# Two MoE stages at batch 1: raw-stream routers, split gather and sums, and the second expert pair's first 4 MB in the dense ring

## The reference, cut to what matters

```python
hn = rms_norm(h, norm_ffn[i])
h = h + hier_moe(hn, ...)
# hier_moe: group router top-1 of 4, expert router top-2 of the 8 in that group
p_group = softmax(xf @ wr_g + br_g);  pg, gi = top_k(p_group, 1)
e_logits = (xf @ wr_e + br_e).reshape(T, 4, 8)
e_in = e_logits of group gi;  pv, pi = top_k(softmax(e_in), 2)
gates = pg * pv / sum(pv)
# every chosen expert e, on its tokens x:  y = (silu(a) * b) @ w_down[e],  a, b = split(x @ w_gu[e])
# out[token] = sum over its two experts of gate * y
```

## Time and profile before

| | |
|---|---|
| median of 3 runs | 2223.04 us (2218.72 to 2226.03) |
| the profiled execution | 2214.99 us |
| its span, first to last instruction | 2213.1 us |
| first MoE stage, from the first `project` to the sums' end | 951.19 to 1434.74 us |
| second MoE stage, the same | 1712.05 to about 2193.8 us |
| PE, share of the span | 94% |
| granted TensorE clock, mean | 0.982 of 2.4 GHz |

### The profile page before, as it was taken

How to read it: one execution, slowest core, us unless ns; L and a number is a source line. 1 busy time by engine, 2 the same in 40 slices (tenths; PEclk the granted TensorE clock), 3 DMA queues, 4 the chain that set the end, 5 groups by cost and what they waited for, 6 DMA issues and landing times.

```text
span 2213.1 us, 38037 instructions
## 1 busy us (share of the span) xinstructions
PE 2089.7 (94%) x15784; PEld 1525.4 (69%) x15785; DVE 892.3 (40%) x1468; ACT 669.1 (30%) x958; POOL 79.6 (4%) x118
## 2 busy tenths in 40 slices
PE   7997899998999998989999999999998999999998
PEld 5876899988999897844454444588987444444444
DVE  5866678745643544521111111165275111111112
ACT  3434464253652466311111111144342011111111
POOL 0100111101000200000000000000000000000000
PEclk9998999999999999999999999999999999999999
DMA  9731389803655251779999999535631899999993
GB/s 361 262 129 48 139 306 333 317 31 115 228 176 187 77 191 41 288 287 421 422 422 422 422 422 422 226 115 190 247 148 77 356 419 422 422 422 422 422 422 126
DMA packets 108084, 603.26 MB, mean 273 GB/s; under 512 B 10062, under 2 KB 10500, under 8 KB 58836
## 3 DMA queue, kind: packets, MB, share of 16 engines
q1 hardware_dynamic: 95872, 559.39, 63.9%
q0 software_dynamic: 11840, 42.34, 5.3%
q10 hardware_dynamic: 276, 0.13, 0.0%
HBM read 600.73 MB, written 1.05 MB: 272 GB/s over the span
## 4 chain that ended last, share of the span: by engine, by line
PE 88%; DVE 4%; ACT 4%; issue 2%; DMA 2%; SPq 0%; DVEq 0%; ACTq 0%
PE bank L939 20%; PE bank L951 10%; PE bank L551 10%; PE bank L552 10%; PE bank L553 10%; PE bank L923 6%; PE bank L970 5%; PE bank L581 4%; DMA dense_w<-in_w_in 1%; PE bank L561 1%; PE bank L562 1%; PE bank L560 1%; PE bank L594 1%; PE bank L631 1%; DVE work L1514 1%
## 5 line engine op out<-in xcount | busy, mean ns | idle before, releaser
L939 PE MATMUL bank<-expert_w,work 128*32 128x512 f32 (+1 forms) x4032 | 447.7, 594 | 24.0 <-issue 21.5
L939 PEld LDWEIGHTS bank<-expert_w,work 128*32 128x32 f32 (+1 forms) x4032 | 156.1, 110 | 314.2 <-issue 314.2
L434 DVE TENSOR_TENSOR w_low<-dense_w,w_high 128x2048 fp32r<-128x2048 f32 x112 | 256.1, 2290 | 221.5 <-ACT w_high L427 220.8
L427 ACT ACTIVATE w_high<-dense_w 128x2048 fp32r<-128x2048 f32 x120 | 228.6, 1911 | 312.1 <-DMA dense_w<-in_mlp_w 195.1
L951 PE MATMUL bank<-expert_w,work 128*32 128x512 f32 (+1 forms) x2016 | 226.4, 594 | 0.0
L2075 DVE TENSOR_TENSOR work<-work,bank 128x512 f32<-128x512 f32 x32 | 22.0, 688 | 400.3 <-ACT work L1404 400.3
L951 PEld LDWEIGHTS bank<-expert_w,work 128*32 128x32 f32 (+1 forms) x2016 | 63.5, 110 | 144.5 <-issue 144.5
L923 PEld LDWEIGHTS bank<-work 128*128 128x128 f32 x1088 | 133.1, 199 | 33.9 <-issue 33.8
L551 PE MATMUL bank<-u_pairs_mlp,w_high 128*128 128x256 f32 x512 | 145.2, 284 | 6.0 <-ACT u_pairs_mlp L1140 6.0
L923 PE MATMUL bank<-work 128*128 128x128 f32 x1088 | 139.2, 287 | 6.9 <-issue 6.9
L551 PE MATMUL bank<-hidden_pairs,w_high 128*128 128x256 f32 x512 | 144.9, 283 | 0.0
(11 more groups left out here) (379 smaller groups left out, 3620.8 us busy)
## 6 DMA issues: line engine op xcount, KB each, us to landing
expert_w<-in_expert_w_gu SPq DMA_DIRECT2D x256, 1024.0 KB, 13.1
expert_w<-in_expert_w_down SPq DMA_DIRECT2D x128, 1024.0 KB, 9.6
dense_w<-in_mlp_w SPq DMA_DIRECT2D x64, 1024.0 KB, 5.5
dense_w<-in_ret_w_in SPq DMA_DIRECT2D x24, 1024.0 KB, 5.4
u<-in_ada_w POOLq DMA_DIRECT2D x40, 512.0 KB, 6.2
work<-in_ada_w POOLq DMA_DIRECT2D x40, 512.0 KB, 6.9
dense_w<-in_fox_w_in SPq DMA_DIRECT2D x16, 1024.0 KB, 5.0
dense_w<-in_w_in SPq DMA_DIRECT2D x12, 1024.0 KB, 8.1
```

Source lines behind the costliest of these rows:

```text
L427: nc.scalar.activation(HIGH_OF[at], dense_w[:, at % RING], ACT.Copy, scale=scale).then_inc(S("w_high_ready"), 1)
L434: ins = nc.vector.tensor_tensor(w_low[:, at % RING], dense_w[:, at % RING], high, ALU.subtract)
L939: last = mm(free[half][cols, :], rows[:, k, cols], pieces[:, k // 2, a, k % 2, half * 512:(half + 1) * 512], start=k == 0, stop=k == KT - 1)
```

## The change

1. **Raw-stream routers.** The norm ahead of the router goes. `router_w` is multiplied once by the norm's gains (DVE, during the forgetting attention), PE multiplies h itself, and DVE scales the logits by the reciprocal deviation, which ACT now sums per token from the turned h. The gains for the experts are applied when `xg` leaves PSUM (`ffn_gain`, a new small table that GpSimd loads early).
2. **Split gather.** The turned, scaled stream is written as `hn_high` (ACT) and `hn_low` (DVE), both fp32r, and `pick` is fp32r; the gather is 32 fp32r matmuls in the place of 16 plain ones.
3. **Split sums.** The expert output is scaled by each slot's gate as it leaves PSUM, into `y_high` (ACT, two halves) and then `y_low` (DVE, two halves); `pickT` is 0/1. `add_up` is 16 fp32r matmuls in the place of 8 plain ones. `take_pick_wT` is now a sum over columns (the gates, `slot_w`) and a comparison.
4. **4 MB ahead.** Pieces 0 and 1 of pair 1 are loaded into the dense ring ahead of the loop; round 1 of `project` reads them there, in its own branch. Pieces 0 and 1 in `expert_w` take pair 2's weights when round 0 has used them. From round 2 on the loop refills as before. `ret_in`'s first four chunks come behind the loop.
5. The WARM matmuls of the MoE heads go, and `pick_w`'s arithmetic moves behind the first gather.

The diff, cut to its core:

```diff
-        hn_tok = part(wk, 0, TT, D)
+        hn_high = parts("hn_high", "work", 0, [TT, D])
+        hn_low = parts("hn_low", "u", 0, [TT, D])
...
+            def load_ahead(l):
+                for j in range(2):
+                    for a in range(2):
+                        sp.dma_start(dense_w[:, 2 * j + a].rearrange("p r n -> p (r n)"), rows_of(l, 1, j, a)).then_inc(S("expert_ahead"), 16)
...
-                if l == 0:
-                    for j in range(RING):
-                        load(chunk("ret_in", 0, j))
-                with sp.Fori(1, PAIRS) as i:
+                load_ahead(l)
+                for pair in range(2):
+                    for j in range(PIECES // 2):
+                        if (pair, j) in ((1, 0), (1, 1)):
+                            continue
+                        sp.wait_ge(expert_used, PIECES * (PAIRS * l + pair) + 2 * j + 2)
+                        load_experts(l, pair + 2 if j < 2 else pair + 1, j, 2 if j < 2 else 1)
+                with sp.Fori(3, PAIRS) as i:
...
                     for k in range(4 * half, 4 * half + 4):
                         for tt in range(TT):
-                            last = mm(free[2 + half][:, (k % 4) * P:(k % 4 + 1) * P], every_other(hn_tok[:, tt], k),
-                                      source[:, tt, :], start=tt == 0, stop=tt == TT - 1)
+                            for x in (hn_high, hn_low):
+                                last = mm(free[2 + half][:, (k % 4) * P:(k % 4 + 1) * P], every_other(x[:, tt], k), source[:, tt, :],
+                                          start=tt == 0 and x is hn_high, stop=tt == TT - 1 and x is hn_low)
...
+                    with pe.If(i == 1):
+                        pe.wait_ge(S("expert_ahead"), 64 * (l + 1))
+                        for k in range(4):
+                            block_of(k, lambda a: dense_w[:, k // 2 * 2 + a])
+                    with pe.If(i != 1):
+                        for k in range(4):
+                            both_in(k, loaded)
+                            block_of(k, lambda a: pieces[:, k // 2, a])
...
                     for k in range(KT):
-                        last = mm(total[k // 2][:, (k % 2) * SEQ:(k % 2 + 1) * SEQ], y_sb[:, k * P:(k + 1) * P],
-                                  pick_wT.rearrange("p t n -> p (t n)"), start=False, stop=False)
+                        for y in (y_high, y_low):
+                            last = mm(total[k // 2][:, (k % 2) * SEQ:(k % 2 + 1) * SEQ], y[:, k * P:(k + 1) * P], pickT,
+                                      start=False, stop=False)
...
-                for _ in range(WARM):
-                    mm(free[3][:, 0:SEQ], ident, K("rope_cos"), start=True, stop=True)
...
                 def take_xg(rows, done):
-                    fn(rows[:, 0:4, :], free[2][:, :].rearrange("p (k n) -> p k n", k=4), ACT.Copy).then_inc(done, 1)
+                    for k in range(4):
+                        last = fn(rows[:, k, :], free[2][:, k * P:(k + 1) * P], ACT.Copy, scale=ffn_gain[:, KT * l + k:KT * l + k + 1])
+                    last.then_inc(done, 1)
...
                 def take_y(done):
-                    fn(y_sb[:, 0:512], free[2][:, :], ACT.Copy).then_inc(done, 1)
+                    for half in range(2):
+                        fn(y_high[:, half * 512:(half + 1) * 512], free[2 + half][:, :], ACT.Copy, scale=slot_w).then_inc(done, 1)
...
                 def take_pick_wT(done):
-                    V.tensor_copy(pick_wT, free[1][:, 0:SEQ].rearrange("p (t n) -> p t n", t=TT)).then_inc(done, 1)
+                    V.tensor_reduce(slot_w, free[1][:, 0:SEQ], AX.X, ALU.add)
+                    V.tensor_scalar(pickT, free[1][:, 0:SEQ], 0.0, None, ALU.is_gt).then_inc(done, 1)
+                def take_y(made, at, done):
+                    for half in range(2):
+                        dve.wait_ge(made, at + half + 1)
+                        eight = slice(half * 512, (half + 1) * 512)
+                        last = V.scalar_tensor_tensor(y_low[:, eight], free[2 + half][:, :], slot_w, y_high[:, eight].bitcast(f32),
+                                                      ALU.mult, ALU.subtract)
```

More of the change, by code:

```diff
@@ L257, in build @@
         hidT = part(wk, 5120, 4, P)
-        y_sb = part(wk, 5632, D)
-        pick = part(wk, 6656, TT, P)
+        y_high = parts("y_high", "work", 5632, [D])
+        y_low = parts("y_low", "work", 9728, [D])
+        pick = parts("pick", "work", 6656, [TT, P])
         pick_w = part(wk, 6912, TT, P)
-        pick_more = part(wk, 7168, TT, P)
+        pick_more = parts("pick_more", "work", 7168, [TT, P])
         pick_w_more = part(wk, 7424, TT, P)
-        pick_wT = part(wk, 7680, TT, P)
+        pickT = parts("pickT", "work", 7680, [TT * P])
+        slot_w = small[:, 92:93]
         is_first = part(wk, 7936, TT, P)
@@ L502, in _ @@
                 if l == 0:
-                    for at in range(chunk("ret_in", 1, 0), chunk("ret_out", 0, 0)):
+                    for at in range(chunk("ret_in", 0, 0), chunk("ret_out", 0, 0)):
                         load(at)
@@ L896, in experts @@
                 mm(bank(t)[:, 2 * E:3 * E], K("ones"), pick_e[:, 2, 1, :], start=False, stop=True).then_inc(tile_ready, 1)
[L898 to L902, removed]
+                take_h(2)
+                take_h(3)
                 for q in range(4):
@@ L931, in tiles_of, with project, block_of @@
                     return [(slice(at, at + UNIT), int(at >= first)) for at in range(0, P, UNIT)]
-                def project(rows, loaded, used=None, first=SLOTS):
-                    for k in range(KT):
-                        both_in(k, loaded)
+                def project(i, rows, loaded, used=None, first=SLOTS):
+                    def block_of(k, piece):
                         for half in range(2):
                             for cols, a in tiles_of(first):
-                                last = mm(free[half][cols, :], rows[:, k, cols], pieces[:, k // 2, a, k % 2, half * 512:(half + 1) * 512],
+                                last = mm(free[half][cols, :], rows[:, k, cols], piece(a)[:, k % 2, half * 512:(half + 1) * 512],
                                           start=k == 0, stop=k == KT - 1)
@@ L942, in project @@
                             last.then_inc(used, 1)
+                        return last
+                    with pe.If(i == 1):
[6 more added lines that the diff above has]
+                            block_of(k, lambda a: pieces[:, k // 2, a])
+                    for k in range(4, KT):
+                        both_in(k, loaded)
+                        last = block_of(k, lambda a: pieces[:, k // 2, a])
                     return last
@@ L1018, in experts @@
                         with pe.If(first_rows == first):
-                            project(xg, loaded, expert_used, first)
+                            project(i, xg, loaded, expert_used, first)
                     pe.wait_ge(S("pick_ready"), count + 1)
@@ L2139, in experts @@
                     take_pick_wT(S("pick_wT_ready"))
-                    dve.wait_ge(expert_used, PIECES * n + PIECES)
-                    take_y(S("y_dve"))
+                    take_y(S("y_act"), 2 * ((PAIRS + 1) * l + i + 1), S("y_dve"))
                 for q in (1, 3):
@@ L2147, in experts @@
                     wait_evac(dve, TILES[f"combine_{l}"] + q)
-            for n in range(8):
-                wait_evac(dve, TILES["fox_out"] + n)
             experts(0)
@@ L2210, in _ @@
             add_to_h("ret_out")
-            for n in range(8):
-                wait_evac(dve, TILES["ret_out"] + n)
             experts(1)
```

149 lines of the change are left out of this document (95 added, 54 removed).

## The result

The changed kernel takes 2936.45 us (median of 4 runs, 2934.01 to 2942.5), the kernel before 2220.88 (4 runs of the same session, 2213.29 to 2226.03). The ratio is 1.323, 95% interval 1.3197 to 1.3263: slower by 716 us. The prediction of 2190 had the wrong sign, and its range ended at 2262.

A forecast was written before the change was run, and what follows sets the result against it. The prediction took PE's own work to bound the expert loops, by a hair ahead of the weight transport. Loops -27.4 and heads -6 gave -33.4, taking 2223.04 to 2190 us, with a range of 2172 to 2262.

The forecast's parts named there:

- rival D: `project`'s longer code no longer stays at hand; each round pays half of about 4 us, 64 us, about 2250; chance 0.04.
- Sums: In the expert loop's round: 16 fp32r matmuls take 1.92 us instead of 3.46, 1.54 less a round.
- Gather: In the expert loop's round: 32 fp32r matmuls take 3.84 us instead of 3.96, 0.13 less a round.
- rival A: In the gather, narrow fp32r matmuls cost as much as plain ones: 3.98 us more a round, 2295 (milder 2262); chance 0.17.
- The loop's gain: Expert loops: PE's round 27.89 us, transport's 29.84; PE waits near pair 7; 13.7 us gained a stage, 27.4 for both.
- 4 MB ahead: At the expert loop's start: one round's queue growth saved, 1.95 us a stage, already inside the loop's gain.
- The heads: Before each layer's first `project`: no norm, WARM or memsets in the path; 3 us off each, -6, between 0 and -12.
- ACT and DVE in the round: `take_xg` and `take_y` end some 1.4 us later, covered by `project`: nothing, or 1.4 a round without that cover.
- the last round: Behind the last round, no cover: 1.4 us more for the copies, against 1.7 saved in the last sums.
- `ret_in`: Four chunks moved behind the loop: first lands 2.5 us later; costs nothing, up to 5 with a queue 10 us longer.
- the scaling of the router: Once, on DVE: under 0.8 us, where it next waits 4.24 for ACT; costs nothing.
- The sum: Whole kernel: -27.4 for the loops and -6 for the heads, -33.4 together, from 2223.04 to 2190 us.

The follow-up runs named there:

- experiment 10: The changed kernel with the dense-ring choice only in the `project` copy that round 1 takes, and the WARM matmuls back: 2536.41 us, ratio 1.1426.
- 5: The kernel before with 48 plain matmuls in PE's loop behind a branch never taken: 2553.41 us.
- experiment 8: The changed kernel without the 4 MB ahead, with the WARM matmuls back before the first gather: 2195.01 us, ratio 0.9872.
- 12: The kernel before with the split sums alone, keeping its normed router, plain gather and WARM matmuls: 2200.56 us, ratio 0.9911.
- 11: The changed kernel without the 4 MB ahead, with the WARM matmuls back and a plain gather: 2184.67 us, ratio 0.9841.
- Experiment 13: The kernel of experiment 10 with 40 small instructions more at PE's start, nothing else changed: 2205.97 us, ratio 0.9934.
- 7: The changed kernel with the dense-ring choice only in the `project` copy that round 1 takes: 2205.39 us, ratio 0.9931.
- 1: The changed kernel without the 4 MB ahead, with `project` and SP's loop as before: 2206.19 us, ratio 0.9946.
- 9: The kernel before with 72 never-run matmuls in PE's loop and 160 small instructions at PE's start: 2519.81 us.

## Why the prediction was wrong

**The step that failed** is the place of the loop's code in the sum. The sum has no term for it: "the new branches in `project` lengthen that code" is priced in the heads alone, and for the rounds there is only rival D, "The round's code no longer stays at hand". Its mechanism was named and its two numbers were wrong. The price was "half" of one first pass, 2 us a round; measured are 54.3 - 28.1 = 26.2 us a round: 13.8 more at the edge and 6.2 ahead of the gather while code comes in, and 6.2 more because PE then works on a low clock (project 16.02 for 13.94, gather 7.06 for 3.92, turns 1.32 for 0.77, sums 2.36 for 1.91). The chance was 0.04, for which the only evidence was that "in the 13 rounds before there is no such wait". That shows that the old loop fits, and says nothing on how near it is to not fitting: 137 more instructions (experiment 10) or 195 (5) were enough. The order of the instructions showed `project` growing; I put no number on the loop's size.

**Sums.** Right: 1.92 us forecast, 1.91 measured.

**Gather.** Right: 3.84 forecast, 3.92 measured against 3.96 in the kernel before. The floor under 256 columns held. The sign by which I wanted to know rival A, "if the gather takes over 5.5 us (A)", was a bad one: it took 7.06, and the cause was the clock. It needed the granted clock beside it. The Trainium skill (TensorE: Matmul & The Clock Gate, Why this matters for your kernels) warns of idle gaps between bursts of matmuls; the granted clock of 0.50 in the gather behind 6.23 us without work agrees with it, and there the price of the gather rose from 3.92 to 7.06 us.

**The loop's gain.** Without the holes the paces are right and the gain is too high. `project` starts 28.06 us apart (27.89 forecast), later the transport sets 29.82 (29.84 forecast). In experiment 8 PE waits for `expert_w` from about round 9 of layer 0 on, where I had "near pair 7". From there the last quarter of `project` waits for the fourth refill, which lands some 25.4 us after its issue in round after round, as forecast (start us, us, what):

```profile
1200.05 25.35 DMA expert_w<-in_expert_w_gu
1225.54 3.67 PE bank L960 x16
1229.87 25.36 DMA expert_w<-in_expert_w_gu
```

Without the 4 MB ahead my terms give 13.7 - 1.95 = 11.8 us a stage. Experiments 12 and 11 measure 11.9 and 8.4, 11.1 and 9.5: 20.3 and 20.6 of 23.6. 8 has 8.2 and 5.4: its first rounds take 36.1 and 37.2 us where 12's take 32.4 and 33.1. In layer 0 the wait for code there is the same (3.46 and 3.45 us), but the gather behind it takes 6.39 us at a granted clock of 0.57 in 8 and 12's, a plain one, 4.01 at 1.00.

**4 MB ahead.** Forecast a gain of 1.95 us a stage. Experiment 13 against 8 has stages of 477.5 and 478.2 against 475.0 and 476.0: a loss of 2.5 and 2.2. The gain is there: in layer 0 the four rounds from the ninth on, in which 8 waits for weights, take 114.0 us in 13 and 118.4 in 8. But the branch makes the edge 0.92 us instead of 0.51 in each round in which PE sets the pace, and the first pass through the longer code is dearer (first round 40.4 us instead of 36.1, head 0 4.0 us longer). The intervals of the two ratios, 0.991 to 0.9958 and 0.9853 to 0.989, don't overlap. With the WARM matmuls in, this part of the change loses some 10 us even where its code fits. Without them no loss shows: 7 has 0.9931 (0.9914 to 0.9949) and 1 has 0.9946 (0.992 to 0.9973). That pair is a poor one, because 1 has the early holes of layer 0.

**The heads.** Forecast -6 for both, between 0 and -12. With the WARM matmuls left in, the raw router gives 5.4 and 8.7 us (8) or 5.9 and 9.0 (11): 14.9, beyond my best case. Without them, as in the change, it gives 3.1 and 6.5 (1), 9.6 in all and inside the range, and the first `project` then takes 16.6 and 16.8 us instead of 14.1 and 15.4. That takes 3.9 us of it back. In the changed kernel itself the heads give 0.3 and 3.1: the holes in the new code, 4.76 us ahead of the first `project`, eat the rest.

**ACT and DVE in the round, the last round, `ret_in`, the scaling of the router.** No cost of theirs shows in any run, and none was tried by itself. ACT waits 62.5 us in all for `ret_in` in experiment 7 and 60.3 in the kernel before. The openings of the profiled executions differ: the same matmul of the first block's transform starts at 464.3 us in the kernel before, at 468.2 and 475.5 with 24 and 48 dead matmuls, at 474.3 in experiment 11. That is why the medians and not single spans carry the comparisons of experiments 8, 11, 12 and 13.

**The sum.** What I described, with a loop short enough, is experiment 7: 2205.39, where I had 2190. Its stages gain 3.5 and 1.5 us where I had 13.7 each, because its edges are 0.9 us where the kernel before has 0.51, and its first rounds take 42.1 and 42.4 us where that has 36.4 and 34.2; its heads gain 2.8 and 3.2. The change as made is that plus its stages, 850.3 + 825.5 against 479.7 + 479.9, or 22.4 us a round (26.2 where PE set the pace, less where the transport would have had it wait anyway), and 2.6 us in the heads: 719 of the 731. The 2190 was nearer to experiment 8 (2195.01), which keeps the WARM matmuls and leaves out the 4 MB; that is luck, as two terms were off in opposite ways (stages 13.6 for 27.4, heads 14.1 for 6).

**Still open:** what sets the count of seven blocks, where the count of blocks starts, and why the early rounds of layer 0 in experiment 1 took three passes until the holes ended (3.94, 4.34 and 4.46 us, one packet of instructions in each) where its layer 1 took one; that stage has 493.2 us for it. The profiled execution, 2220.75, is one of four of 2214 to 2223 us; the other six took 2195 to 2208, and no profile tells whether they had these holes.

## What to carry to other kernels

A loop's code is a resource like its buffers: count its instructions in the compiled program, with the branches not taken, ahead of any change that copies a block of it, because in these runs the steady rounds paid nothing up to the limit and 20 to 26 us each, on 28, behind it. Where it stands counts too: instructions anywhere ahead of the loop can push it over. Where rows of "issue" and packets of the instruction queue appear in a steady loop, put never-taken code into the old kernel: one run tells code from data. And a slow group of matmuls is read with its granted clock beside it, or a hole's cost is taken for the price of the instruction behind it.

## What the hardware showed that I had not expected

- In these runs PE keeps a loop's code at hand if it touches at most seven blocks of 256 instructions (experiments 7, 9, 13); at eight or nine, it loads about nine packets in every round, not one (272 more packets in 30 rounds of the changed kernel). The 30 loops of the 15 kernels fit this, from 1457 to 1872 instructions.
- So the same kernel is 2536 or 2206 us by 40 instructions at its start that do nothing (10 and 13), and filler matmuls for the clock can cost 330 us by moving a loop (7 to 10).
- In the changed kernel one round of such loading costs 20 us of waiting and 6 of low clock. 32 fp32r matmuls of 128 columns take 3.92 us at a granted clock of 1.00 and 7.06 at 0.50.
